# The last two experts of a routed SwiGLU: high and low parts of the tokens side by side in one stationary block

## What is computed

```python
def moe_swiglu(h, w_router, w_gate, w_up, w_down):
    logits = (x @ w_router).astype(jnp.float32)
    top_logit, top_idx = lax.top_k(logits, TOP_K)        # 2 of 8 experts a token
    gates = jax.nn.softmax(top_logit, axis=-1)
    ...
    # for the tokens xb of expert e, with F = 3584 hidden columns:
    #   (jax.nn.silu(xb @ w_gate[e]) * (xb @ w_up[e])) @ w_down[e]
    out = jnp.zeros((T, D), h.dtype).at[rows_token].add(ys * rows_gate[:, None])
```

## Time and profile before

| | |
|---|---|
| median of 3 runs | 1447.54 us (1447.46 to 1451.54) |
| the profiled execution | 1448.84 us, span 1447.0 us |
| experts, from the first expert's rows to the end | about 970 us of the span |
| busy share of the span | PE 98%, DVE 77%, ACT 65% |
| moved by DMA | 446.72 MB, of it 336 slots of experts |

### The profile page before, as it was taken

One profiled execution on the slowest core, in us unless ns is written; L12 is line 12 of the kernel. 1 busy time (PEld: TensorE's weight loads), 2 busy tenths in 40 slices (PEclk: granted clock), 3 DMA queues, 4 the chain that ended last, 5 costly groups with the idle time before them and its releaser, 6 DMA issues.

```text
span 1447.0 us, 19532 instructions
## 1 busy us (share of the span) xinstructions
PE 1417.0 (98%) x7348; PEld 1201.7 (83%) x7348; DVE 1116.4 (77%) x865; ACT 944.6 (65%) x866; POOL 52.8 (4%) x78
## 2 busy tenths in 40 slices
PE   8999999999998999999999999999999999999997
PEld 8887999998887888888888888888888888888886
DVE  5565544546775888798888889879888888987987
ACT  5654544335664867787677777767768768677774
POOL 1000100000000500000000000000000000000002
PEclk9999999999999899999999999999999999999999
DMA  9743665555531699999999999999999999999993
GB/s 283 265 146 116 252 228 187 193 191 177 185 117 59 213 397 395 397 393 395 393 354 395 396 346 394 398 349 392 396 391 347 395 393 346 393 398 352 396 396 136
DMA packets 205253, 446.72 MB, mean 309 GB/s; under 512 B 8448, under 2 KB 42400, under 8 KB 205200
## 3 DMA queue, kind: packets, MB, share of 16 engines
q1 hardware_dynamic: 200144, 428.34, 80.5%
q0 software_dynamic: 5056, 17.66, 3.5%
HBM read 432.86 MB, written 13.11 MB: 308 GB/s over the span
## 4 chain that ended last, share of the span: by engine, by line
PE 90%; DVE 3%; ACT 3%; DMA 2%; issue 1%; SPq 1%; DVEq 0%; ACTq 0%
PE ps L1686 28%; PE ps L1688 28%; PE ps L1687 28%; PE ps L2300 2%; DMA raw<-in_w_exp_down_dram 1%; DMA raw<-in_w_mem_kv_dram 1%; ACT w_hi L593 1%; ACT e_whi L977 1%; DVE w_lo L1058 1%; PE ps L2243 0%; PE ps L1835 0%; PE ps L2294 0%; ACT sc L637 0%; DVE small L1105 0%; PE ps L1712 0%
## 5 line engine op out<-in xcount | busy, mean ns | idle before, releaser
L1567 DVE TENSOR_TENSOR e_wlo<-raw,e_whi 128x2048 fp32r<-128x2048 f32 x336 | 752.6, 2286 | 103.0 <-ACT e_whi L977 102.9
L977 ACT ACTIVATE e_whi<-raw 128x2048 fp32r<-128x2048 f32 x336 | 622.9, 1915 | 53.2 <-PE ps L1688 26.2
L1686 PE MATMUL ps<-e_whi,act_hi 128*128 128x512 f32 x1344 | 529.4, 394 | 0.7 <-DVE act_lo L1580 0.7
L1688 PE MATMUL ps<-e_wlo,act_hi 128*128 128x512 f32 x1344 | 523.9, 390 | 0.0
L1687 PE MATMUL ps<-e_whi,act_lo 128*128 128x512 f32 x1344 | 523.2, 389 | 0.0
L1688 PEld LDWEIGHTS ps<-e_wlo,act_hi 128*128 128x128 f32 x1344 | 252.3, 188 | 53.3
L1686 PEld LDWEIGHTS ps<-e_whi,act_hi 128*128 128x128 f32 x1344 | 252.4, 188 | 52.0 <-DVE e_wlo L1567 1.4
L1687 PEld LDWEIGHTS ps<-e_whi,act_lo 128*128 128x128 f32 x1344 | 252.6, 188 | 50.6
L1058 DVE TENSOR_TENSOR w_lo<-raw,w_hi 128x2048 fp32r<-128x2048 f32 (+3 forms) x69 | 148.7, 2167 | 118.8 <-ACT w_hi L593 118.5
L593 ACT ACTIVATE w_hi<-raw 128x2048 fp32r<-128x2048 f32 (+3 forms) x69 | 124.3, 1816 | 47.2 <-PE ps L1688 43.5
L982 ACT ACTIVATE act_hi<-ps 128x512 fp32r<-128x512 f32 x56 | 33.5, 598 | 155.2 <-PE ps L2300 155.2
(11 more groups left out here) (270 smaller groups left out, 966.1 us busy)
## 6 DMA issues: line engine op xcount, KB each, us to landing
raw<-in_w_exp_gate_dram SPq DMA_DIRECT2D x112, 1024.0 KB, 9.3
raw<-in_w_exp_up_dram SPq DMA_DIRECT2D x112, 1024.0 KB, 9.5
raw<-in_w_exp_down_dram SPq DMA_DIRECT2D x112, 1024.0 KB, 10.1
raw<-in_w_dense_gate_dram SPq DMA_DIRECT2D x11, 1024.0 KB, 5.3
raw<-in_w_dense_up_dram SPq DMA_DIRECT2D x11, 1024.0 KB, 5.6
raw<-in_w_dense_down_dram SPq DMA_DIRECT2D x11, 1024.0 KB, 6.7
raw<-in_w_out_dram SPq DMA_DIRECT2D x8, 1024.0 KB, 5.0
raw<-in_w_in_a_dram SPq DMA_DIRECT2D x7, 1024.0 KB, 11.9
```

What stands on the lines that cost most here:

```text
L977: nc.scalar.activation(e_whi[:, (s - NPRE) % E_SPLIT, :], raw[:, s % RAW, :], ACT.Copy)\
L1567: nc.vector.tensor_tensor(e_wlo[:, r, :], raw[:, s % RAW, :], e_whi[:, r, :].bitcast(F32), ALU.subtract).then_inc(lo_ready, 1)
L1686: nc.tensor.matmul(dst, l_hi, r_hi, start=start, stop=False)
L1688: return nc.tensor.matmul(dst, l_hi, r_lo, start=False, stop=stop)
```

## The change

The experts are put in an order by their number of tokens: expert 0 stays first, then the others from the most tokens to the fewest. The last two (`FIRST_LIGHT` is 6) get at most 64 tokens each, and take another path, in which the 128 rows of the stationary block hold the high parts of up to 64 tokens and beside them their low parts. A matmul by the high part of the weights and one by their low part then give all products, two a group in place of three; the rows of a token's high and low part are added later, by a multiplication with `fold` (two identities of 64 above each other). If one of the two had more than 64 tokens, `flag` would call for the second sweep.

```diff
+                def light_product(e, u0, bank, first=False):
+                    for half in range(2):
+                        hi, lo = slot(e, u0 + half, 4, 512)
+                        if first:
+                            pe.wait_ge(xg_packed, 2 * (e - FIRST_LIGHT) + half + 1)
+                        for kk in range(4):
+                            k = 4 * half + kk
+                            nc.tensor.matmul(bank, xg_hi[:, k, :], hi[:, kk, :], start=k == 0, stop=False)
+                            ins = nc.tensor.matmul(bank, xg_hi[:, k, :], lo[:, kk, :], start=False, stop=k == KT - 1)
+                        ins.then_inc(slot_used, 1)
+                def light_turn(e, j):
+                    pe.wait_ge(e_silu, e * STEPS + j + 1)
+                    pe.wait_ge(e_hr, e * STEPS + j + 1)
+                    for i, src in enumerate((e_h, e_u)):
+                        for m in range(4):
+                            to = 256 * i + LIGHT * m
+                            ins = nc.tensor.matmul(ps[:, 4, to:to + LIGHT], src[:, P * m:P * m + P], fold, start=True, stop=True)
+                    ins.then_inc(e_tr, 1)
...
+                def fold_rows():
+                    pe.wait_ge(y_raw, 2)
+                    for n in range(2):
+                        ins = nc.tensor.matmul(ps[0:LIGHT, 5 + n, :], fold, y_tok[:, 512 * n:512 * n + 512], start=True, stop=True)
+                    ins.then_inc(y_folded, 1)
```

In a step of the light path ACT and DVE first copy gate and up bank to SBUF as they are (`e_h` and `e_u`), TensorE folds and turns both (`light_turn`), and only then ACT takes silu (`light_silu`), DVE multiplies (`light_product`), ACT makes the high part (`light_high`) and DVE the low part (`light_low`). On ACT:

```diff
+                def light_silu(e, j):
+                    act.wait_ge(e_tr, e * STEPS + j + 1)
+                    nc.scalar.activation(s_T, ps[:, 4, 0:256], ACT.Silu)\
+                      .then_inc(l_silu, 1)
+                def light_high(e, j):
+                    act.wait_ge(l_prod, (e - FIRST_LIGHT) * STEPS + j + 1)
+                    nc.scalar.activation(h_hi[j % 2][:, :, 0:LIGHT], h_T.rearrange("p (m n) -> p m n", m=4), ACT.Copy)\
+                      .then_inc(e_hi, 1)
...
-                        if j == 0 and sweep == 0:
+                        if j == 0 and folded:
+                            evacuate_rows(e, signal=y_raw)
+                        elif j == 0 and sweep == 0:
                             evacuate_rows(e)
...
                             split_slots(e, gate_end(j) + 2, 2)
-                            hidden(e, j - 1)
+                            (light_silu if light else hidden)(e, j - 1)
...
-                        nc.scalar.activation(e_h[:, :], ps[:, j % 2, :], ACT.Silu).then_inc(e_silu, 1)
+                        nc.scalar.activation(e_h[:, :], ps[:, j % 2, :], ACT.Copy if light else ACT.Silu).then_inc(e_silu, 1)
+                        if light and j > 0:
+                            light_high(e, j - 1)
+                        if j == 0 and folded:
+                            act.wait_ge(y_folded, 1)
+                            evacuate_rows(e, rows=LIGHT)
 
                         split_slots(e, gate_end(j + 1) - 2, 2)
```

and on DVE:

```diff
+                def light_product(e, j):
+                    dve.wait_ge(l_silu, (e - FIRST_LIGHT) * STEPS + j + 1)
+                    nc.vector.tensor_tensor(h_T, s_T, ps[:, 4, 256:512], ALU.mult)\
+                      .then_inc(l_prod, 1)
+                def light_low(e, j):
+                    dve.wait_ge(e_hi, e * STEPS + j + 1)
+                    nc.vector.tensor_tensor(h_hi[j % 2][:, :, LIGHT:P], h_T.rearrange("p (m n) -> p m n", m=4),
+                                            h_hi[j % 2][:, :, 0:LIGHT].bitcast(F32), ALU.subtract).then_inc(e_lo, 1)
...
+                        if j > 0 and light:
+                            split_slots(e, gate_end(j) + 2, 2)
+                            light_product(e, j - 1)
+                            split_slots(e, gate_end(j + 1) - 2, 1)
+                            light_low(e, j - 1)
+                            split_slots(e, gate_end(j + 1) - 1, 1)
...
+                        if light:
+                            nc.vector.tensor_copy(e_u, ps[:, 2 + j % 2, :]).then_inc(e_hr, 1)
```

More of the change, by code:

```diff
@@ L125, in trunk @@
         flag = sb("flag", [1, 8], I32)
-        sb("act_pad", [P, 24])
+        places = sb("act_pad", [P, 24])
+        order_of = places[:, 0:8].bitcast(U32)
+        place, is_light = places[:, 8:16], places[:, 16:24]
         act_hi = sb("act_hi", [P, KT, S], F32R)
@@ L430, in expert_loads, with loads @@
                 base = NPRE + sweep * NE * PER_EXPERT
-                with sp.Fori(0, NE) as e:
+                def loads(e, x):
                     u = 0
@@ L1004, in expert @@
                         split_slots(e, PER_EXPERT, 1)
-                    hidden(e, STEPS - 1)
+                    if light:
+                        light_silu(e, STEPS - 1)
+                        light_high(e, STEPS - 1)
+                    else:
+                        hidden(e, STEPS - 1)
                     if not last:
@@ L1015, in experts @@
                 gathered(sweep, 0, range(1, 2))
-                with act.Fori(0, NE - 1) as e:
+                heavy = FIRST_LIGHT if sweep == 0 else NE - 1
+                with act.Fori(0, heavy) as e:
                     expert(e, False)
-                expert(NE - 1, True)
+                for e in range(heavy, NE):
+                    expert(e, e == NE - 1)
             act.wait_ge(slot_used, NPRE)
@@ L1477, in _ @@
             link(nc.vector.memset(flag[:, :], 0))
+            nc.vector.tensor_tensor(fold, ident[:, 0:LIGHT], ident[:, LIGHT:P], ALU.add).then_inc(fold_ready, 1)
             out_b_sums(0)
@@ L1584, in column, with pack @@
                     return table[:, :, e:e + 1] if isinstance(e, int) else table[:, :, bass.ds(e, 1)]
+                def light_product(e, j):
[6 more added lines that the diff above has]
+                                            h_hi[j % 2][:, :, 0:LIGHT].bitcast(F32), ALU.subtract).then_inc(e_lo, 1)
+                def pack(e, half):
+                    dve.wait_ge(xg_l, 2 * e + half + 1)
+                    ks = slice(4 * half, 4 * half + 4)
+                    nc.vector.tensor_copy(xg_hi[:, ks, LIGHT:P], xg_lo[:, ks, 0:LIGHT].bitcast(F32)).then_inc(xg_packed, 1)
                 def expert(e, last):
+                    light = sweep == 0 and isinstance(e, int)
+                    for half in (range(2) if light else ()):
+                        pack(e, half)
                     for j in range(STEPS):
@@ L1624, in expert @@
                         split_slots(e, PER_EXPERT, 1)
-                    hidden(e, STEPS - 1)
+                    if light:
+                        light_product(e, STEPS - 1)
+                        light_low(e, STEPS - 1)
+                    else:
+                        hidden(e, STEPS - 1)
                     if not last:
@@ L1639, in experts @@
                     gathered(sweep, 0)
-                with dve.Fori(0, NE - 1) as e:
+                heavy = FIRST_LIGHT if sweep == 0 else NE - 1
+                with dve.Fori(0, heavy) as e:
                     expert(e, False)
-                expert(NE - 1, True)
+                for e in range(heavy, NE):
+                    expert(e, e == NE - 1)
                 return remainder_y, add_tile
@@ new lines, in light_turn, with light_down @@
+                def light_turn(e, j):
[6 more added lines that the diff above has]
+                    ins.then_inc(e_tr, 1)
+                def light_down(e, j, u0, parts=range(2), by_column=False):
+                    pe.wait_ge(e_lo, e * STEPS + j + 1)
+                    for half in parts:
+                        hi, lo = slot(e, u0 + half, 2, D)
+                        for m, n in ((0, 0), (1, 0), (0, 1), (1, 1)) if by_column else ((0, 0), (0, 1), (1, 0), (1, 1)):
+                            f = 2 * half + m
+                            ns = slice(512 * n, 512 * n + 512)
+                            nc.tensor.matmul(ps[:, 5 + n, :], h_hi[j % 2][:, f, :], hi[:, m, ns], start=j == 0 and f == 0,
+                                             stop=False)
+                            ins = nc.tensor.matmul(ps[:, 5 + n, :], h_hi[j % 2][:, f, :], lo[:, m, ns], start=False,
+                                                   stop=j == STEPS - 1 and f == 3)
+                            if by_column and (m, n) == (1, 0):
+                                ins.then_inc(last_down, 1)
+                        ins.then_inc(slot_used, 1)
@@ L2337, in expert @@
                             scatter(e + 1, 1)
-                        if j == 2 and (sweep or last):
-                            pe.wait_ge(oh_ready, 2 * e + n_oh + 2 if sweep else 4)
+                        if j == 2 and sweep:
+                            pe.wait_ge(oh_ready, 2 * e + n_oh + 2)
                             for t in range(TT):
@@ L2360, in expert @@
                         last_slot(e, STEPS - 1, PER_EXPERT - 1)
-                with pe.Fori(0, NE - 1) as e:
+                heavy = FIRST_LIGHT if sweep == 0 else NE - 1
+                with pe.Fori(0, heavy) as e:
```

(3 more changed lines are left out.)

127 lines of the change are left out of this document (103 added, 24 removed).

## The result

The changed kernel takes 1476.1 us (median of 4 runs, 1471.3 to 1477.2) where the kernel before took 1447.7 beside it: ratio 1.0186, interval 1.0172 to 1.0201. Measured twice more beside other kernels, it took 1469.5 (ratio 1.0148, 1.0131 to 1.0165) and 1471.6 us (1.0168, 1.0147 to 1.0189). It is slower, by 1.5 to 1.9%. The profiled execution took 1471.27 us, its span is 1469.4, 22.4 more than before.

What follows compares the result with a forecast made beforehand. PE was taken to bound the kernel before, DVE's waits for ACT the light steps after; terms -1.9, +5.2, +2.7, +5.0, +1.2, +2.9 sum to +15.1 us on a 1447.0 span, forecast 1462, range 1445 to 1482.

Steps and rivals of the forecast that it cites:

- its sum: Terms added along DVE's operations that end a step: +15.1 us, forecast 1462, own range 1454 to 1470, chance 0.64.
- the case of the clock: Rival: in the light steps PE waits 5 us and its clock falls; 1464 to 1522 us, chance 0.14.
- the border: From `e_u` of expert 6's last step to expert 7's first `e_u`, with the fold: +2.7 us (2 to 4).
- The exchange: Light steps: DVE waits for ACT's split, queued behind `light_high`; 2.3 us lost a step, making steps of 16.8 us.
- The rival in which half of it is hidden: ACT and DVE hide half of the 2.3 us per step; 15 us saved, the kernel even at 1448, chance 0.13.
- the faster one: Rival: light experts bound by loads, DVE–ACT handover free and fold hidden; 1434 us, chance 0.09.
- the turn: PE's eight small matmuls in each light step, estimated at 1.0 us.
- mild end: Clock returns within the first two slots: nothing lost in the steps, 2 us at the border and the end.
- The reserve of 3 us: In a light step, PE has the turn ready some 3 us before ACT needs it.
- Routing: Fifteen linked operations of `choice_inverse` before expert 0's split make the rest +2.9 us later (bounds 1 to 3.4).
- The end: After expert 7's last `e_u`, down to the copy of the gates and what follows: +1.2 us.
- the start of expert 6: From PE finishing expert 5 to expert 6's first `e_u`, with two light gate slots: -1.9 us.

Runs made afterwards that it cites:

- Mending that one order: Changed kernel with ACT splitting one slot before `light_high` in the light steps; 1450.9 us, ratio 1.0025.
- the stand-ins alone: Kernel before the change, plus fifteen small linked DVE operations in `choice_inverse`, as many as the new routing has; 1454.7 us, ratio 1.0049.
- both orders mended and the routing early: Changed kernel with one split ahead of `light_high`, folded copies behind the splits of slots 4 and 5, routing operations behind expert 0's first split; 1444.9 us.
- half the loads: The kernel with both orders mended and the routing early, loading only half of every slot in the two light experts; 1436.5 us, ratio 0.9921.

## Why the prediction was right, and where its sum was short

The forecast was slower, with 1462 us and a range of 1445 to 1482; the time lies inside, 8 to 14 us above the forecast. By the prediction's own division it isn't its sum that was hit: that had a range of 1454 to 1470, and only one of the three medians (1469.5, 1471.6, 1476.1) lies in it, at its edge. They lie in the case of the clock (1464 to 1522), near its lower end. The direction and the main cause were right, and the nearness of the number isn't luck, since the terms can be checked one by one; but four of them were too small by 7 us in the first profile, most of it at the border.

**The exchange: right, in place and size.** DVE idles 2.28 or 2.29 us behind each product, 2.3 was worked out; steps of 16.85, 16.83 was. Mending that one order takes 19 to 25 us off. The rival in which half of it is hidden has fallen, and so has the faster one, in which it costs nothing. "PE waits 4.9 us a step" and "PE some 70% busy" were wrong: PE is 87% busy, with a wait of 2.1 to 2.3 us in most steps. Of the missing 2.7 us, 1.6 are eight matmuls at half the clock (0.43 from one to the next in place of 0.23), and most of the rest is the turn, 1.7 us in place of 1.0. The one step of the first profile in which the clock stayed up has a wait of 3.84.

**The clock: rival and sum came true together, and this is the term that the sum lacked.** The sum had the clock at nothing. The text kept it as another case, of 0.14, whose mild end was right in kind: "If the clock comes back within the first two slots, nothing is lost in the steps and 2 us at the border and the end". It falls in every light step of the first profile but the one from 1393.57 and the last, each time for 3.4 us or more. In the steps of expert 6 it costs nothing, but by a hair: the silu ends at 1239.15 (1238.76 and 0.39), and DVE needs it at 1239.17; in the next four steps 0.10 to 0.16 us are left. The reserve of 3 us that the prediction gave the turn is all used up. Two steps of expert 7 lose 1.2 and 0.8 us. They are the two of that expert ahead of which PE had waited longest, 4.90 and 3.84 us, so that the clock was low from its first matmul on and the turn began 10.1 and 9.9 us behind that matmul, where most steps have 9.0; DVE waits 0.94 us for ACT in the first of them:

```profile
1371.15 0.42 DVE L1666 TENSOR_TENSOR H<-H,ps 128x256 f32<-128x256 f32 x1 [0.94 <-ACT H L1011]
```

The Trainium skill, TensorE: Matmul & The Clock Gate, section "HAM oscillation — how this bites in real kernels", describes a clock that falls in each round of a loop with short bursts and longer waits; here the trace shows it falling in nearly each step with bursts several times as long as the visible wait.

**The border: mis-sized, +2.7 against +7.0 and +5.2.** The prediction had PE at the new gate slots 9.4 us behind `e_u`; it was there after 13.2, with the turn at the low clock (3.7 us against an estimate of 1.0 and 1.7 to its end) and the last down slots and the turn of rows (1.9 against 1.03) behind it. From there on it was right: 16.1 us to the next `e_u` predicted, 16.6 measured (1343.88 - 1327.26), the fold 1.93 against 1.5. With the fold's copies moved, and the turn at the full clock, PE is there after 9.8, close to the 9.4 predicted, and the rest takes 10.8 us: the fold's place on ACT costs 5.8 us, about twice the length of the fold and its copies (1.93 and 1.07).

**Routing: right where the clock stayed up, else a lower bound.** The distance in expert 0 says 2.9, 3.8 and 2.9 for the changed kernel, 5.0 for the stand-ins alone. The +2.7 and +3.1 of the table are near 2.9 in part by luck, since the start of expert 0 moves by a microsecond between profiles. The reason given ("no other reserve there") was right; that PE waits meanwhile and comes back slow was not seen.

**The end: +1.2 against +2.0 to +4.2.** The part between is again the turn: DVE waits 1.38 or 2.76 us for its silu.

**The other estimates:** the start of expert 6 came out at -1.8 (-1.9), SP's reading of the expert's number nowhere in the waits. The turn is 16 instructions, each float32 matmul standing as two in the trace, and takes 1.7 to 2 us at the full clock, not 1.0.

**Where PE's 76 us went.** With both orders mended and the routing early the kernel gains 3 us on before, 11 with half the loads. The reason stands in the rows of before: six steps took 95.8 and 96.0 us there, since PE's 16.8 a step was mixed with steps of 14.4. By DVE's own work, 14.7 a step, six steps can't take less than 88.2, 15 us less in both experts; by the loads, 15.94 a step, they take 95.6 once the ring's lead is used up, and that is almost no gain. The measured 90.2 and 98.1, and 90.4 and 91.9 with half the loads, fit this but for some 2 to 4 us, the late turns.

## What to carry to other kernels

When two engines that each work in order pass one small value back and forth, write down what each has queued behind its half. A split of 1.9 us standing behind an operation of 0.4 cost some 2 us in each of twelve steps, and one changed place in the order of one engine gave 19 us or more back. A cheaper bottleneck also idles more, and here that made it slow: price the small operations behind the idle time at both clocks, and ask how much reserve is left then. And before taking work from one engine, work out the step by each of the others, loads included: here 16.8 us a step on PE stood against 14.7 on DVE and 15.9 for the loads, which left little to win.

## What the hardware showed

- Behind waits of PE of 2.1 to 2.3 us the granted clock fell only after PE had taken up work again: the first matmul behind a wait of 2.12 us starts at 1244.57, and those from 1245.13 on start 0.43 us apart, until 1248.54 (the slow stretch of the step before had ended at 1231.2). In the other steps of the first profile it fell 0.8 to 1.9 us behind the first matmul, and in one, from 1393.57 on, not at all. Behind the waits of 3.84, 4.90, 5.29 and 7.11 us in these two experts the first matmul already ran at the low clock. In a step of 16.85 us some 3.4 ran at the low clock. PE in the changed kernel:

```profile
1231.20 0.52 PE L2446 MATMUL ps<-e_whi,act_hi 128*128 128x512 f32 x1
1231.56 0.39 PE L2448 MATMUL ps<-e_wlo,act_hi 128*128 128x512 f32 x1
...
1242.06 0.39 PE L2425 MATMUL ps<-e_wlo,act_hi 128*128 128x512 f32 x1
1244.57 0.50 PE L2446 MATMUL ps<-e_whi,act_hi 128*128 128x512 f32 x1 [2.12 <-DVE act_hi L1671]
1244.90 0.43 PE L2448 MATMUL ps<-e_wlo,act_hi 128*128 128x512 f32 x1
1245.13 0.63 PE L2446 MATMUL ps<-e_whi,act_hi 128*128 128x512 f32 x1
...
1248.54 0.39 PE L2446 MATMUL ps<-e_whi,act_hi 128*128 128x512 f32 x1
1248.77 0.39 PE L2448 MATMUL ps<-e_wlo,act_hi 128*128 128x512 f32 x1
...
1410.41 0.80 PE L2446 MATMUL ps<-e_whi,act_hi 128*128 128x512 f32 x1 [3.84 <-DVE act_hi L1671]
```

- The wait that shows is short in part because the slow stretch fills 1.6 us of the gap that fewer matmuls leave: 2.1 to 2.3 us with it, 3.84 in the step without it. A profile that is read by waits alone hides this; the pitch of matmuls and the granted clock show it.
- Loads of 1 MB reached 397 GB/s over 92.5 us, with a DMA share of 1.04, in a stretch in which ACT waited for them (both orders mended, routing early).
- A small matmul in float32 is two instructions in the trace: the turn, eight matmuls of 64 columns, is 16 of them and takes 1.7 to 2 us at the full clock and 3.7 at the low one.
